# The norm in front of the head projections: gain multiplied ahead of the root, last residual and squares in pieces, one low part on GpSimd

## The reference

```python
def rmsnorm(x, g):
    xf = x.astype(jnp.float32)
    y = xf * lax.rsqrt(jnp.mean(xf * xf, axis=-1, keepdims=True) + EPS)
    return (y * g).astype(x.dtype)

def second_block(...):
    h = x
    for l in range(DEPTH):
        h = h + 0.5 * swiglu(rmsnorm(h, ffn1_norm[l]), ffn1_w_in[l], ffn1_w_out[l])
        h = h + hybrid_mixer(rmsnorm(h, mix_norm[l]), w_in[l], ...)
        ...
```

## Time and profile before

| | us |
|---|---|
| median of 3 runs | 1368.71 (1368.55 to 1368.86) |
| profiled execution | 1368.36 |
| its span, first to last instruction | 1366.5 |
| TensorE busy | 1353.6 (99%) |
| VectorE busy | 1042.8 (76%) |
| ScalarE busy | 802.8 (59%) |
| GpSimd busy | 29.5 (2%) |

### The profile page before, as it was taken

The page is one execution under the profiler, slowest core; times in us unless marked ns, Lnnn a source line. Parts: engine busy times, 40 slices in busy tenths (PEclk is TensorE's granted clock), DMA queues, the critical chain, the costliest instruction groups (busy, mean ns, idle before and its releaser), DMA issues.

```text
span 1366.5 us, 24310 instructions
## 1 busy us (share of the span) xinstructions
PE 1353.6 (99%) x8590; PEld 1209.4 (89%) x8590; DVE 1042.8 (76%) x1621; ACT 802.8 (59%) x1312; POOL 29.5 (2%) x72
## 2 busy tenths in 40 slices
PE   8999999999999999999999999999999999999998
PEld 7888888989888888888899999999999998988887
DVE  5798888777666686666778888888888877666665
ACT  4445554644443364444668898898898854544444
POOL 7000000000000010000000000000000000000000
PEclk9999999999999999999999999999999999999999
DMA  8575554655555756666574553554543286566661
GB/s 267 153 194 159 151 144 152 202 196 191 185 189 196 228 155 187 185 184 194 150 203 110 132 158 96 146 144 113 141 130 123 80 211 204 172 206 197 193 185 62
DMA packets 291213, 227.79 MB, mean 167 GB/s; under 512 B 10882, under 2 KB 270164, under 8 KB 291156
## 3 DMA queue, kind: packets, MB, share of 16 engines
q1 hardware_dynamic: 291012, 226.75, 55.8%
q10 hardware_dynamic: 144, 0.26, 0.1%
HBM read 225.90 MB, written 1.08 MB: 166 GB/s over the span
## 4 chain that ended last, share of the span: by engine, by line
PE 95%; DVE 2%; ACT 1%; DVEq 0%; issue 0%; DMA 0%; POOL 0%; ACTq 0%; SPq 0%; POOLq 0%
PE M L2078 10%; PE G L2078 9%; PE M L2066 8%; PE M L2067 7%; PE M L2068 7%; PE G L2061 5%; PE G L2063 5%; PE G L2062 5%; PE M L2080 5%; PE G L2080 5%; PE G L2204 2%; PE G L2962 2%; PE M L2771 1%; PE M L2789 1%; PE G L2066 1%; PE G L2068 1%
## 5 line engine op out<-in xcount | busy, mean ns | idle before, releaser
L1214 DVE TENSOR_TENSOR w_lo<-w_raw,w_hi 128x2048 fp32r<-128x2048 f32 (+2 forms) x248 | 479.0, 1935 | 132.8 <-ACT w_hi L654 128.7
L654 ACT ACTIVATE w_hi<-w_raw 128x2048 fp32r<-128x2048 f32 x197 | 376.0, 1909 | 168.9 <-PE M L2080 54.1
L2061 PE MATMUL G<-xa,w_hi 128*128 128x256 f32 x592 | 176.8, 299 | 0.0
L2063 PE MATMUL G<-xa,w_lo 128*128 128x256 f32 x592 | 167.2, 282 | 0.0
L2062 PE MATMUL G<-xa,w_hi 128*128 128x256 f32 x592 | 167.0, 282 | 0.0
L2078 PE MATMUL M<-xa,w_hi 128*128 128x512 f32 x600 | 151.6, 394 | 0.0
L2078 PE MATMUL G<-xa,w_hi 128*128 128x512 f32 x568 | 142.4, 393 | 0.0
L2078 PEld LDWEIGHTS M<-xa,w_hi 128*128 128x128 f32 x600 | 107.8, 189 | 19.8
L2078 PEld LDWEIGHTS G<-xa,w_hi 128*128 128x128 f32 x568 | 104.0, 188 | 21.3 <-issue 1.2
L2066 PE MATMUL M<-w_hi,xb 128*128 128x512 f32 x300 | 117.3, 391 | 0.1
L2067 PE MATMUL M<-w_lo,xb 128*128 128x512 f32 x300 | 117.1, 390 | 0.0
(11 more groups left out here) (449 smaller groups left out, 2546.8 us busy)
## 6 DMA issues: line engine op xcount, KB each, us to landing
w_raw<-in_w_in SPq DMA_DIRECT2D x150, 512.0 KB, 4.7
w_raw<-in_ffn_w_in SPq DMA_DIRECT2D x88, 512.0 KB, 5.1
w_raw<-in_w_ff SPq DMA_DIRECT2D x64, 512.0 KB, 4.3
w_raw<-in_ffn_w_out SPq DMA_DIRECT2D x44, 512.0 KB, 4.9
w_raw<-in_w_in SPq DMA_DIRECT2D x33, 256.0 KB, 3.2
w_raw<-in_w_out SPq DMA_DIRECT2D x16, 512.0 KB, 4.1
w_raw<-in_w_branch_gdn SPq DMA_DIRECT2D x16, 512.0 KB, 5.3
w_raw<-in_w_branch SPq DMA_DIRECT2D x12, 512.0 KB, 4.2
```

The costliest lines, as they stand in the source:

```text
L654: nc.scalar.activation(w_hi[:, slot, :], w_raw[:, slot, :], ACT.Copy).then_inc(hi_ready, 1)
L1214: return v.tensor_tensor(dst, src, hi.bitcast(F32), ALU.subtract)
L2061: mm(out_, w[0], x[0], start=first, stop=False)
L2063: return mm(out_, w[1], x[0], start=False, stop=last_)
```

## The change

Five things are done at the norm between `ffn1` and the heads, and two counts are adapted to them.

- The last two chunks of `ffn1` are multiplied with `halves_apart`: on block 1 both chunks are added to the first half, then both to the second. The number of matmuls is the same.
- The second half of the last residual is summed in two pieces of 256 columns, each of which raises `summed1`. ScalarE squares them one by one, with a mean carried on from piece to piece, into a spare row.
- VectorE does the first half of the last residual ahead of the product of block 0.
- The gain is multiplied into block 1 ahead of the root, in two halves, and the root is multiplied in behind it by an instruction that reads one tensor.
- GpSimd makes the low part of `heads` chunk 0, whole, when its high part is there; VectorE no longer does.

```diff
@@ gpsimd
+        c = FIRST["heads"]
+        slot = c % RING
+        pool.wait_ge(hi_ready, c + 1)
+        pool.wait_ge(lo_ready, c)
+        nc.gpsimd.tensor_tensor(w_lo[:, slot, :], w_raw[:, slot, :], w_hi[:, slot, :].bitcast(F32), ALU.subtract
+                                ).then_inc(lo_ready, 1)
@@ scalar
         rms_first(summed0, 1)
         split(c0 + 31 + RING)
-        rms_half(half_summed, 1)
-        rms_rest(summed1, 1)
+        spare_row = ffr[:, 0:2, :].rearrange("p b c -> p (b c)")
+        act.wait_ge(half_summed, 1)
+        nc.scalar.activation(spare_row[:, 0:512], res[:, 1, 0:512], ACT.Square, accum_out=stat[:, 46:47])
+        settle()
+        nc.scalar.activation(stat[:, 47:48], stat[:, 46:47], ACT.Identity, scale=1.0 / D, bias=eps[:, 1:2])
+        act.wait_ge(summed1, 1)
+        nc.scalar.activation(spare_row[:, 512:768], res[:, 1, 512:768], ACT.Square, accum_out=stat[:, 41:42])
+        settle()
+        nc.scalar.activation(stat[:, 48:49], stat[:, 41:42], ACT.Identity, scale=1.0 / D, bias=stat[:, 47:48])
+        act.wait_ge(summed1, 2)
+        nc.scalar.activation(spare_row[:, 768:D], res[:, 1, 768:D], ACT.Square, accum_out=stat[:, 49:50])
+        settle()
+        nc.scalar.activation(stat[:, 43:44], stat[:, 49:50], ACT.Ln, scale=1.0 / D, bias=stat[:, 48:49])
+        settle()
+        nc.scalar.activation(stat[:, 45:46], stat[:, 43:44], ACT.Exp, scale=-0.5).then_inc(rms_rstd[1], 1)
         x_hi(3)
@@ vector
-        sum_and_norm(3, c0 + 33, 0.5, 4, gain_mix, lambda: w_low_half(c0 + 31 + RING, 0))
+        for h, (lo_, hi_) in enumerate(halves):
+            dve.wait_ge(y_first, 2 * 3 - 1 + h)
+            ins = residual(0, lo_, hi_, 1.0, 0.5)
+        ins.then_inc(summed0, 1)
+        dve.wait_ge(y_half, 3)
+        residual(1, 0, 512, 1.0, 0.5).then_inc(half_summed, 1)
+        rms_apply_first(4, gain_mix)
+        settle()
+        v.tensor_tensor(tmp[:, 1, 0:512], res[:, 1, 0:512], gain_mix[:, 0:512], ALU.mult)
+        dve.wait_ge(gemm_done, c0 + 33)
+        for lo_, hi_ in ((512, 768), (768, D)):
+            residual(1, lo_, hi_, 1.0, 0.5).then_inc(summed1, 1)
+        settle()
+        v.tensor_tensor(tmp[:, 1, 512:D], res[:, 1, 512:D], gain_mix[:, 512:D], ALU.mult)
+        settle()
+        dve.wait_ge(rms_rstd[1], 2)
+        for h, (lo_, hi_) in enumerate(halves):
+            v.tensor_scalar(tmp[:, 1, lo_:hi_], tmp[:, 1, lo_:hi_], stat[:, 45:46], None, ALU.mult
+                            ).then_inc(half_normed if h == 0 else normed1, 1)
         x_low(3)
-        w_low_half(c0 + 31 + RING, 1)
+        dve.wait_ge(lo_ready, FIRST["heads"] + 1)
         w_low(c0 + 32 + RING)
@@ tensor, last_rows of ffn
-            last_rows([...], [...], down_ready)
+            last_rows([...], [...], down_ready, halves_apart=second == "late")
```

More of the change, by code:

```diff
@@ L1191, in _ @@
         rms_half(half_summed, 2)
-        rms_rest(summed1, 2)
+        rms_rest(summed1, 3)
         split(c0 + 3 + RING)
@@ L1197, in _ @@
         rms_half(half_summed, 3)
-        rms_rest(summed1, 3)
+        rms_rest(summed1, 4)
         settle()
@@ L2540, in down_ready @@
                 pe.wait_ge(h_ready, h0 + STEPS - 2 + 2 * n)
-            last_rows([(c0 + 31 + n) % RING for n in range(2)], [x_rows(xb_hi, xb_lo, r) for r in (2, 0)], down_ready)
+            last_rows([(c0 + 31 + n) % RING for n in range(2)], [x_rows(xb_hi, xb_lo, r) for r in (2, 0)], down_ready,
+                      halves_apart=second == "late")
         ffn(FIRST["ffn1"], EV_FFN1, H_FFN1, 2, 3, 1, "late")
```

## The result

| | before | changed |
|---|---|---|
| median of 8 runs, us | 1368.70 (1368.23 to 1369.38) | 1373.56 (1372.65 to 1374.40) |
| profiled execution, us | 1368.36 | 1374.28 |
| its span, us | 1366.5 | 1372.5 |

The change makes the kernel slower: ratio 1.0036, 95% interval 1.0027 to 1.0045, or 4.9 us. Its eight runs lie 1.75 us apart, those of before 1.15.

A forecast was written before the change was run, and what follows sets the result against it. TensorE, 95% of the chain, was taken as the bound. GpSimd's hold on VectorE makes the transposes of block 1 3.3 us later: 1368.71 + 3.3 = 1372.0 us, range 1370.3 to 1374.6.

The forecast's parts named there:

- The hold: At the norm, GpSimd's subtraction blocks VectorE's product of the gain from about 674.5 until 678.54 us.
- three records of before: Mask-building and large-subtraction rows where VectorE and GpSimd overlap; read as excluding each other, whole instruction by whole instruction.
- Size of the wait: Transposes of block 1 start at 679.86 instead of 676.57, 3.3 us later; possible loss 3.1 to 4.4.
- Root near 677.1 to 677.8, not the last wait: ScalarE's root at the norm comes 1.3 to 2.0 us later than before, but VectorE's held product ends later still.
- the sixth from the end: Last matmul of the third group, starting at 671.86; behind it the first chunk's count rises, at 672.25.
- VectorE first: Rival, chance 0.05: product of the gain runs before GpSimd; loss 3.4 us if the one-tensor product is held too.
- Side by side: Rival, chance 0.10: GpSimd does not hold VectorE, the root decides, TensorE 1.1 to 1.7 us late, about 1370.0.
- The clock: Rival, chance 0.05: the granted clock falls after TensorE's 3.7 us wait, costing 1.8 to 3.7 us more, 1373.8 to 1375.7.
- the argument from the first 4.71 us: Against a falling clock: TensorE was idle for the first 4.71 us, yet the granted clock of 0 to 5 us is 1.00.
- a PEclk under 9 in the slice of 680: Sign in the new profile that would show the steps wrong.
- the forecast case: VectorE's product held by GpSimd at the norm, chance 0.78, time 1371.8 to 1373.1 us.
- the mask rows: While masks are built, a small GpSimd instruction takes 2.43 us instead of 0.24; read as a record containing its wait.

The follow-up runs named there:

- gpsimd_alone: Kernel before with one part of the change: GpSimd makes the low part of heads chunk 0, VectorE's two halves out; 1370.22 us, ratio 1.0016.
- half_on_gpsimd: Changed kernel with only the first half of the heads chunk 0 low part on GpSimd, the second half on VectorE; 1370.10 us, ratio 1.0013.
- low_on_dve: Changed kernel with the low part of heads chunk 0 made whole by VectorE again, GpSimd doing nothing there; 1369.82 us, ratio 1.0010.
- more_spin: Changed kernel with five matmuls without use instead of two ahead of the transposes of block 1; 1371.66 us, ratio 1.0024.
- gpsimd_between: Changed kernel with GpSimd's subtraction held back until VectorE's product with the gain on the second half has ended; 1373.68 us, ratio 1.0039.

## Why the prediction came out as it did

- *Direction and mechanism: right, and shown.* The hold was forecast from three records of before. The changed kernel, gpsimd_alone, half_on_gpsimd and low_on_dve show it by its presence, its length and its absence.
- *Size of the wait: 3.3 forecast; 3.46 in the profile, 3.3 in the time of more_spin.* Link by link, less the 0.59 of the later layer: rounding from 672.35 (672.29 forecast), GpSimd from 674.35 (674.27) for 4.51 (4.47), end of the held product at 679.41 (679.23), transposes at 680.03 (679.86).
- *Root near 677.1 to 677.8, not the last wait: right.* It was there at 677.04, just under the low end; a square of 256 columns takes 0.40, against 0.61 for 512. (The matmul that the prediction calls the sixth from the end is the seventh; its time is the right one.)
- *VectorE first, at about the same price if the one-tensor product is held: right.* In gpsimd_between the transposes of block 1 come 6.75 behind the first ones, 3.63 more than before, where the rival had 3.4; its 1373.68 has the low clock in it as well.
- *Side by side: wrong,* by every run in which GpSimd's subtraction met one of these products.
- *The clock: wrong, and the term that was left out of the sum.* The prediction gave a fall 0.05. It came, with 1.98 us in the profile, in the rival's 1.8 to 3.7, and 1.6 in the median, just under them. The step that failed is the argument from the first 4.71 us. The 1.00 in the earlier trace rows is no measured clock: the trace of the kernel before has no record of the granted clock ahead of 7.41 us, and a window without a record shows 1.00. The matmuls tell the clock there. The rows below give the shortest, middle and longest transpose in ns: behind the idle start of the kernel before, then in the low stretch of the changed kernel, then at its 1.00:

```profile
L2172 PE MATMUL M<-ident,res x4: 421/421/421, 5.2 to 5.8; 128*128 128x128 f32 x4
L2209 PE MATMUL M<-ident,arena x4: 421/422/476, 680.6 to 681.3; 128*128 128x128 f32 x4
L2209 PE MATMUL M<-ident,arena x7: 270/273/273, 674.0 to 674.7; 128*128 128x128 f32 x7
```

So TensorE ran at its lower level behind the idle start, and the row spoke for the rival, not against it. The Trainium skill's rule that an idle array falls to its lower level (TensorE: Matmul & The Clock Gate, section "What's actually happening"), which the prediction set aside for that row, agrees with this trace: 0.50 behind the wait of 3.8 us. The sign named for this, a PEclk under 9 in the slice of 680, did not show: the slice is 34 us long, and its mean is 0.90. The sum was thus 1.6 us short: 1373.56 lies above the 1371.8 to 1373.1 of the forecast case, and in the range only because the range reached into the clock's case.

## What to carry to other kernels

Work handed to GpSimd is not free for VectorE: in these runs a VectorE instruction with two operands in SBUF, or a one-operand product within SBUF, waited until GpSimd's subtraction, which reads SBUF, was all but done (0.69 became 4.91, 0.47 became 3.07). Put GpSimd's work beside VectorE instructions with an operand in PSUM, which kept their length here. Before a count that releases a buffer is moved to a later matmul, look up what waits for it, and what is queued behind the waiter. Price a TensorE wait of several us at more than its length, for the clock may fall in it or behind it: in the profile of the changed kernel 3.5 us more of waiting cost another 2.0. And before a window of 1.00 is taken for a full clock, compare the length of the matmuls in it.

## What the runs showed of the hardware that was not expected

- The granted clock fell to 0.50 within the wait of 3.8 us in the changed kernel (at 679.1, 1.5 us ahead of its end), and about 1 us behind the end of one of 4.0 in gpsimd_between (at 681.7). Between the layer's end and each of these waits TensorE ran only transposes and two matmuls without use. The clock stayed at 1.00 behind the wait of 2.1 us in the profile of gpsimd_alone, and where five matmuls without use ran in the wait (more_spin).
- At the start of the program TensorE runs at its lower level though the windows show 1.00: the first record of the granted clock is at 7.41 us in the trace of before and at 10.07 in that of the changed kernel, and transposes ahead of it take 421 ns, behind it 270 to 273.
- A one-tensor product within SBUF was held for 2.6 us by GpSimd (3.07 instead of 0.47), although it reads only one tensor. No row of before had shown this.
- A held instruction's record contains its wait, on either engine, as the prediction took from the mask rows: 5.54 and 4.51 are the same subtraction on GpSimd.
